# One product of 512 columns for high weights on high and low input, and one-hots made and scaled by VectorE

## The chip, the core and the metric

One of the cores of a Trainium2 chip runs the whole program. The metric is the device time of one execution in microseconds; the time before is the median of three runs. TensorE multiplies, VectorE (DVE), ScalarE (ACT) and GpSimd (POOL) do the rest, and SyncE issues the transfers. Each engine works off its own queue in order, and engines wait for each other by semaphores.

## What is computed

Two transformer blocks on 256 tokens of width 1024, in float32. The change touches the MLP of the first block and the expert layer (PEER) of the second:

```python
f = jnp.square(jax.nn.relu(u @ w_mlp_in[l])) @ w_mlp_out[l]        # 1024 -> 4096 -> 1024

# peer_ffn: 8 heads, 128 x 128 product keys, 16 experts for each head and token
experts = jnp.take_along_axis(cand_idx, pos, axis=-1)
gates = jax.nn.softmax(top_score, axis=-1)
u = jnp.take(expert_down, ei, axis=0)
act = jax.nn.gelu(jnp.einsum("btd,bthkd->bthk", xi, u), approximate=False)
y = jnp.einsum("bthk,bthkd->btd", gi * act, jnp.take(expert_up, ei, axis=0))
```

## The kernel before

**Units of weights.** All weights come in 465 units of 128 x 1024 numbers. ScalarE rounds a unit to fp32r (the high part, `WH`, `split`), and VectorE, for some units with GpSimd's help, takes the difference (the low part, `WL`). The input of a product is split in the same way; high and low part of one feature group lie side by side, 256 + 256 columns of one tile (`XW` or `GW`, seen as `XH`/`XL` and `GH`/`GL`). `products` makes three products for each of 8 steps: high weights by high input, high weights by low input, low weights by high input, each 256 columns into the same 256 columns of a bank of PSUM. A unit that has gone through sets `unit`; ScalarE or VectorE takes the result from the bank (`evac`), and later work on it is `after`.

**Order.** Every engine walks the same list of units (`SLOTS`) with a clock of four ticks per unit. At the start of a unit, ScalarE and VectorE evacuate the unit before and split the weights of the unit two ahead (`due`); smaller jobs (`..._side`) come in at a fixed unit and tick. `bank_of` says which bank a unit writes: three in turn in the MLP and for expert units 4 to 47, two in turn from expert unit 48 on. TensorE waits until the unit that had the bank before is evacuated (`bank_ready`).

**First layer of the MLP.** Units 57 to 120 (`MLP` to `XA`): 32 hidden blocks ("in") and 32 output units ("out"), four and four in turn. ScalarE takes a hidden block with ReLU, VectorE squares it, ScalarE and VectorE split it into `GH` and `GL`.

**Expert layer.** All 16384 experts are computed for every token: 128 down units (`DN` = 209 on), each giving 128 experts x 256 tokens, go through Gelu (ScalarE) into `ACTS`. During the first 46 of them VectorE is also busy with the top-k of all heads (`topk_side`), which ends with expert numbers and gates; TensorE transposes these ("ids", "gate") for `ET` and `GATE`. From `BUILD` = `DN` + 54 on, in 64 groups of four tokens, one per unit: VectorE compares keys with a counter (`build_hot_side`, both one-hots of four tokens in one operation of 1024 elements, two units ahead), ScalarE scales the second one-hot by the gates (`build_scale_side`), TensorE multiplies the two (`build_side`, four products of 128 columns after the first quarter of the unit), VectorE multiplies the finished experts by the result (`build_fold_side`, 4 x n numbers, n growing from 54 to 117), ScalarE copies it for the experts to come (`build_fill_side`), and GpSimd multiplies the newly evacuated expert unit by what has been filled (`evac`, m = 4 to 256 numbers). Then 128 up units follow with products of 512 columns.

## Time and profile before

| | |
|---|---|
| median of 3 runs | 1549.84 us (1549.16 to 1550.37) |
| the profiled execution | 1550.6 us, span 1548.8 us |
| mean granted TensorE clock | 0.992 of full speed |
| TensorE busy | 1509.2 us, 97% of the span |
| VectorE, ScalarE, GpSimd busy | 1036.5, 841.2, 366.3 us |
| first layer's MLP | about 215 to 403 us |
| expert down units with one-hots being built | about 925 to 1165 us |

The numbers of a row are the start and length of an instruction (or of a merged run of them, "x3"), its engine, the line of the kernel, the operation, what it writes and reads, and in brackets how long its engine had been idle and what ended that. A length includes a tail that overlaps the next instruction: what an instruction costs its engine is the distance to the next start. Line 1700 is VectorE's helper for operations of two tensors, 1266 ScalarE's, 684 TensorE's, 2421 GpSimd's.

### The profile page before, as it was taken

The numbers are of one execution on the slowest core, as the hardware profiler recorded it, in microseconds if no ns is written. First come the engines' busy times: TensorE is split into PE (matmuls) and PEld (weight loads), VectorE is DVE, ScalarE is ACT, GpSimd is POOL, SyncE is SP. The second block draws the span as 40 slices with busy tenths as digits, with TensorE's granted clock in tenths as the row PEclk, the third lists the DMA queues.
The fourth block names the chain that finished last, engine by engine and source line by source line (L and its number), as shares of the span: only waits on it lengthen the run. The fifth ranks groups of instructions, "written<-read, shape, count | busy, mean of one in ns | idle before, by whom it ended". The sixth has DMA issues, their size and how long they took to land.

```text
span 1548.8 us, 29248 instructions
## 1 busy us (share of the span) xinstructions
PE 1509.2 (97%) x11442; PEld 1427.7 (92%) x11442; DVE 1036.5 (67%) x1814; ACT 841.2 (54%) x1647; POOL 366.3 (24%) x397
## 2 busy tenths in 40 slices
PE   7999999999879999999999999999999999999998
PEld 7888999999879999999999999999999888888887
DVE  5666666555578764677999956777774555555554
ACT  4576465444446543554444457777774455445544
POOL 1542420000338653403555520011112000000000
PEclk9999999999999999999999999999999999999999
DMA  8652555655325632355455554444445666666664
GB/s 239 209 168 83 175 171 180 185 182 187 121 88 169 187 112 83 128 185 172 146 178 177 178 180 143 141 137 142 145 137 175 193 192 193 196 193 192 193 196 141
DMA packets 76805, 255.15 MB, mean 165 GB/s; under 512 B 9359, under 2 KB 15325, under 8 KB 76541
## 3 DMA queue, kind: packets, MB, share of 16 engines
q1 hardware_dynamic: 76429, 252.63, 52.1%
q8 instruction: 92, 1.51, 0.4%
q0 software_dynamic: 240, 0.66, 0.2%
q14 instruction: 44, 0.36, 0.1%
HBM read 250.23 MB, written 2.75 MB: 163 GB/s over the span
## 4 chain that ended last, share of the span: by engine, by line
PE 86%; DVE 10%; ACT 1%; issue 1%; POOL 1%; DMA 0%; SPq 0%; POOLq 0%; ACTq 0%; DVEq 0%
PE bank L684 85%; DVE wl L1700 3%; DVE big L1700 2%; ACT wh L1266 1%; DVE big L2266 1%; DVE big L1703 1%; DVE big L2277 1%; DVE big L2273 1%; DVE big L2262 1%; DVE big L2283 1%; DVE big L2270 1%; PE bank L1015 0%; ACT big L1266 0%; POOL wl L2421 0%; DMA big<-in_xT 0%
## 5 line engine op out<-in xcount | busy, mean ns | idle before, releaser
L1700 DVE TENSOR_TENSOR wl<-raw,wh 128x1024 fp32r<-128x1024 f32 (+4 forms) x467 | 540.1, 1158 | 379.4 <-ACT wh L1266 378.2
L1266 ACT ACTIVATE wh<-raw 128x1024 fp32r<-128x1024 f32 (+1 forms) x467 | 489.8, 1052 | 320.3 <-PE bank L684 319.2
L684 PE MATMUL bank<-gw,wh 128*128 128x256 f32 x3504 | 647.2, 286 | 0.0
L684 PEld LDWEIGHTS bank<-gw,wh 128*128 128x128 f32 x3504 | 544.7, 192 | 0.2
L684 PE MATMUL bank<-gw,wl 128*128 128x256 f32 x1752 | 495.9, 283 | 6.0 <-POOL wl L2421 5.9
L684 PEld LDWEIGHTS bank<-gw,wl 128*128 128x128 f32 x1752 | 335.2, 191 | 7.4 <-issue 6.2
L684 PE MATMUL bank<-xw,wh 128*128 128x256 f32 x1696 | 326.2, 293 | 12.2 <-ACT wh L1266 8.3
L684 PE MATMUL bank<-wh,xw 128*128 128x512 f32 x1056 | 325.3, 389 | 0.0
L684 PEld LDWEIGHTS bank<-xw,wh 128*128 128x128 f32 x1696 | 271.5, 197 | 18.9 <-ACT wh L1266 8.6
L2421 POOL TENSOR_TENSOR wl<-raw,wh 128x384 fp32r<-128x384 f32 (+4 forms) x139 | 193.7, 1401 | 303.6 <-ACT wh L1266 303.5
L1266 ACT ACTIVATE big<-bank 128x256 f32<-128x256 f32 (+22 forms) x326 | 118.0, 372 | 252.8 <-PE bank L684 213.8
L684 PE MATMUL bank<-xw,wl 128*128 128x256 f32 x848 | 244.4, 288 | 0.0
L684 PEld LDWEIGHTS bank<-wh,xw 128*128 128x128 f32 x1056 | 198.2, 188 | 41.2
L684 PE MATMUL bank<-wl,xw 128*128 128x512 f32 x528 | 205.4, 389 | 0.0
L684 PEld LDWEIGHTS bank<-xw,wl 128*128 128x128 f32 x848 | 166.8, 197 | 0.9 <-DVE wl L1700 0.9
L2421 POOL TENSOR_TENSOR big<-big 128x256 f32<-128x256 f32 (+14 forms) x116 | 106.6, 930 | 213.1 <-ACT big L1266 187.5
L684 PEld LDWEIGHTS bank<-wl,xw 128*128 128x128 f32 x528 | 99.1, 188 | 20.5
L684 PE MATMUL bank<-big 128*128 128x128 f32 (+8 forms) x952 | 98.6, 270 | 4.7 <-DVE big L1994 2.5
L2421 POOL TENSOR_TENSOR big<-big,misc 128x256 f32<-128x256 f32 (+32 forms) x74 | 37.0, 500 | 251.1 <-ACT misc L1266 251.1
L2421 POOL TENSOR_TENSOR big<-big,cols 128x8 f32<-128x8 f32 (+1 forms) x8 | 11.0, 1374 | 358.2 <-DVE big L2409 347.4
L684 PEld LDWEIGHTS bank<-big 128*128 128x128 f32 (+4 forms) x952 | 84.1, 173 | 10.8 <-issue 3.3
L1266 ACT ACTIVATE big<-big 128x256 f32<-128x256 f32 (+2 forms) x183 | 70.7, 405 | 30.3 <-DVE big L1703 15.4
(142 smaller groups left out, 1117.2 us busy)
## 6 DMA issues: line engine op xcount, KB each, us to landing
raw<-in_wst SPq DMA_DIRECT2D x455, 512.0 KB, 3.8
big<-toeplitz SPq DMA_DIRECT2D x16, 128.0 KB, 4.9
raw<-in_w1k SPq DMA_DIRECT2D x4, 512.0 KB, 4.9
raw<-in_w1v SPq DMA_DIRECT2D x4, 512.0 KB, 4.2
big<-in_xT SPq DMA_DIRECT2D x4, 256.0 KB, 5.9
raw<-in_wst SPq DMA_DIRECT2D x4, 256.0 KB, 5.1
diag_in<-big SPq DMA_DIRECT2D x2, 512.0 KB, 3.3
big<-in_keys SPq DMA_DIRECT2D x1, 1024.0 KB, 5.5
```

What stands on the lines that cost most here:

```text
L684: return e.matmul(o, a, b, start=first, stop=last, skip_group_check=True)
L1266: return e.activation(o, x, f, **kw)
L1700: return e.tensor_tensor(o, a, b, f)
L1703: return e.scalar_tensor_tensor(o, a, s, b, f, g)
L2262: e.max(v[:, 0:8], s).then_inc(*tkD.sent((h, tile, names[0][k])))
L2266: e.match_replace(x, v[:, 0:8], s, -3.0e38).then_inc(*tkD.sent((h, tile, names[1][k])))
L2270: e.max(v[:, 8:16], x).then_inc(*tkD.sent((h, tile, names[2][k])))
L2273: e.max_index(i[:, 0:8], v[:, 0:8], s).then_inc(*tkD.sent((h, tile, names[3][k])))
L2277: e.max_index(i[:, 8:16], v[:, 8:16], x).then_inc(*tkD.sent((h, tile, names[4][k])))
L2283: e.tensor_reduce(p[:, :, h, :], flat(room).rearrange("p (t k i) -> p t k i", t=2, i=16), AX, ALU.add).then_inc(*tkD.sent((h, "red", n)))
L2421: return e.tensor_tensor(o, a, b, f)
```

## The change

`WIDE` names 30 hidden blocks of the MLP (all but the first two) and the last 89 down units. For them `wide_products` makes two products per step: high weights by 512 columns (high and low input at once, into both halves of the bank), and low weights by the 256 high columns into the first half. The halves are then added: in the MLP ScalarE copies the second half, VectorE adds the first and does ReLU and square in one operation; in the expert layer ScalarE copies the second half to `LOWS` (`low_half`), splits the next weights, VectorE adds the copy into the bank, and then ScalarE's Gelu follows. `build_scale_side` is gone: VectorE makes each one-hot of 128 by itself, the second one scaled by the gate in the same operation, one unit ahead. The fold comes after the new one-hots in the order, and now waits for the fill.

```diff
+
+
+
+WIDE = [u for u in HID.values() if u >= MLP + 2] + [u for u in range(DN + 39, UP)]
...
-        HOT = [flat(XW[:, 2 * r:2 * r + 2, :]).rearrange("p (t n i) -> p t n i", n=2, i=128) for r in range(4)]
+        HOT = [XW[:, r, :].rearrange("p (t i) -> p t i", i=128) for r in range(4)]
...
+            if u in WIDE and u < XA:
+                return joined.at(u)
             return evD.at(u) if u in evD.value else evA.at(u)
...
+                def wide_products(u, x):
+
+
+                    wh, wl = WH[:, u % RW, :], WL[:, u % RW, :]
+                    o = banks[bank_of(u)]
+                    bank_ready(u)
+                    e.wait_ge(*hi.at(u))
+                    for k in range(8):
+                        c = half(k)
+                        mm(o[:, :], wh[:, c], x[:, k, :], k == 0, k == 7)
+                        if k == 0:
+                            lo_ready(u)
+                        z = mm(o[:, 0:T], wl[:, c], x[:, k, 0:T], False, k == 7)
+                        if k == 7:
+                            z.then_inc(*unit.sent(u))
+                        if k % 2:
+                            yield
+
...
+                    if u in WIDE:
+                        return wide_products(u, XW if u < XA else GW)
...
-                            e.wait_ge(*fiA.at(g - 2))
+                            e.wait_ge(*foD.at(g - 2))
                         for j in range(4):
-                            e.wait_ge(*vgA.at((g, j)))
-                            mm(b[:, half(j)], HOT[g % 4][:, j, 0, :].bitcast(F32), VG[j]).then_inc(*buP.sent((g, j)))
+                            e.wait_ge(*hotD.at((g, j, 1)))
+                            mm(b[:, half(j)], HOT[g % 4][:, j, :].bitcast(F32), VG[j]).then_inc(*buP.sent((g, j)))
...
-                        act(HT[n % 3], ps, AF.Relu).then_inc(*evA.sent(u))
+                        if u in WIDE:
+                            act(HT[n % 3], b[:, T:2 * T], AF.Copy).then_inc(*evA.sent(u))
+                        else:
+                            act(HT[n % 3], ps, AF.Relu).then_inc(*evA.sent(u))
...
-                        e.wait_ge(*unit.at(u))
+                        if u in WIDE:
+                            e.wait_ge(*joined.at(u))
+                        else:
+                            e.wait_ge(*unit.at(u))
...
+                def low_half(u):
+                    if u - 1 in lowA.value:
+                        e.wait_ge(*joined.at(u - 1))
+                    if u > BUILD:
+                        e.wait_ge(*dnG.at(u - 1 - DN))
+                    e.wait_ge(*unit.at(u))
+                    act(LOWS, banks[bank_of(u)][:, T:2 * T], AF.Copy).then_inc(*lowA.sent(u))
...
-                def build_scale_side():
-                    for g in range(NB):
-                        yield from clock.until(BUILD - 1 + g, 1)
-                        e.wait_ge(*hotD.at(g))
-                        if g == 0:
-                            e.wait_ge(*tkA.at("gate"))
-                        for j in range(4):
-                            if g:
-                                e.wait_ge(*buP.at((g - 1, j)))
-                            act(VG[j], HOT[g % 4][:, j, 1, :].bitcast(F32), AF.Copy,
-                                scale=GATE[:, 4 * g + j:4 * g + j + 1]).then_inc(*vgA.sent((g, j)))
...
-                        e.wait_ge(*foD.at(g))
+                        e.wait_ge(*buP.at((g, 3)))
...
+                    if u - 1 in lowA.value:
+                        low_half(u - 1)
+                        split(due(u))
...
+                    elif u in WIDE and u < XA:
+                        n = MLP_UNITS[u - MLP][1]
+                        x = HT[n % 3]
+                        e.wait_ge(*evA.at(u))
+                        tt(x, ps, x, ALU.add).then_inc(*joined.sent(u))
+                        e.wait_ge(*joined.at(u))
+                        stt(x, x, 0.0, x, ALU.max, ALU.mult).then_inc(*rqD.sent(n))
+                    elif u in WIDE:
+                        e.wait_ge(*lowA.at(u))
+                        tt(ps, ps, LOWS, ALU.add).then_inc(*joined.sent(u))
...
-                        e.wait_ge(*buP.at((g, 3)))
+                        e.wait_ge(*fiA.at(g))
...
                 def build_hot_side():
                     for g in range(NB):
-                        yield from clock.until(BUILD - 2 + g, 1)
+                        yield from clock.until(BUILD - 1 + g, 1)
                         if g == 0:
                             e.wait_ge(*tkA.at("ids"))
+                            e.wait_ge(*tkA.at("gate"))
                             e.wait_ge(*unit.at(DN - 1))
                         if g >= 4:
                             e.wait_ge(*buP.at((g - 4, 3)))
-                        tt(HOT[g % 4], IOTA[:, None, None, :].broadcast_to([128, 4, 2, 128]),
-                           ET[:, :, 4 * g:4 * g + 4].rearrange("p n t -> p t n")[:, :, :, None].broadcast_to([128, 4, 2, 128]),
-                           ALU.is_equal).then_inc(*hotD.sent(g))
+                        for j in range(4):
+                            t = 4 * g + j
+                            e.tensor_scalar(HOT[g % 4][:, j, :], IOTA, ET[:, 0, t:t + 1], None,
+                                            ALU.is_equal).then_inc(*hotD.sent((g, j, 0)))
+                            if g:
+                                e.wait_ge(*buP.at((g - 1, j)))
+                            e.tensor_scalar(VG[j], IOTA, ET[:, 1, t:t + 1], GATE[:, t:t + 1],
+                                            ALU.is_equal, ALU.mult).then_inc(*hotD.sent((g, j, 1)))
```

VectorE while the one-hots are being built, one unit and the start of the next, before (`big<-big,bank` is a fold, `xw<-misc` a comparison, `wl<-raw,wh` a split):

```order
1020 L1700 TENSOR_TENSOR big<-big,bank 128x59x4 [waits down_pool,ev_act,build_pe]
1021 L1700 TENSOR_TENSOR xw<-misc 128x1024 [waits build_pe]
1022 L1700 TENSOR_TENSOR wl<-raw,wh 128x1024 [waits hi]
1023 L1700 TENSOR_TENSOR big<-big,bank 128x60x4 [waits down_pool,ev_act,build_pe]
1024 L1700 TENSOR_TENSOR xw<-misc 128x1024 [waits build_pe]
```

The same place now (`bank<-bank,misc` is the addition of the halves):

```order
1127 L1733 TENSOR_TENSOR big<-big,bank 128x59x4 [waits down_pool,ev_act,fill]
1128 L1733 TENSOR_TENSOR bank<-bank,misc 128x256 [waits low_copied]
1129 L1733 TENSOR_TENSOR wl<-raw,wh 128x1024 [waits hi]
1130 L2400 TENSOR_SCALAR xw<-misc 128x128 [waits build_pe]
1131 L2404 TENSOR_SCALAR misc<-misc 128x128 [waits build_pe]
1132 L2400 TENSOR_SCALAR xw<-misc 128x128
1133 L2404 TENSOR_SCALAR misc<-misc 128x128 [waits build_pe]
1134 L2400 TENSOR_SCALAR xw<-misc 128x128
1135 L2404 TENSOR_SCALAR ones<-misc 128x128 [waits build_pe]
1136 L2400 TENSOR_SCALAR xw<-misc 128x128
1137 L2404 TENSOR_SCALAR ident<-misc 128x128 [waits build_pe]
1138 L1733 TENSOR_TENSOR big<-big,bank 128x60x4 [waits down_pool,ev_act,fill]
```

One comparison has become eight, an addition has come in, and the comparisons stand between split and fold.

ScalarE in the same stage, before (`wh<-raw` rounds weights, `xw,misc` is the scaling, `big<-bank` with three sizes the fill, the rows after it Gelu in two parts):

```order
742 L1266 ACTIVATE wh<-raw 128x1024 [waits unit,load0]
743 L1266 ACTIVATE misc<-xw,misc 128x128 [waits build_pe,hot]
744 L1266 ACTIVATE misc<-xw,misc 128x128 [waits build_pe]
745 L1266 ACTIVATE ones<-xw,misc 128x128 [waits build_pe]
746 L1266 ACTIVATE ident<-xw,misc 128x128 [waits build_pe]
747 L1266 ACTIVATE big<-bank 128x71x4 [waits fold]
748 L1266 ACTIVATE big<-bank 128x240 [waits unit]
749 L1266 ACTIVATE misc<-bank 128x16 [waits down_pool]
```

and now:

```order
781 L1294 ACTIVATE misc<-bank 128x256 [waits unit,down_pool,halves_joined]
782 L1294 ACTIVATE wh<-raw 128x1024 [waits unit,load0]
783 L1294 ACTIVATE big<-bank 128x212 [waits halves_joined]
784 L1294 ACTIVATE misc<-bank 128x44 [waits down_pool]
785 L1294 ACTIVATE big<-bank 128x63x4 [waits build_pe]
```

The four scalings are gone, a copy has come in, and Gelu moved behind the rounding of weights, where it waits for VectorE's addition.

VectorE at the end of top-k (the COPY and the `128x256` operation behind it are the maximum and the subtraction ahead of the exponential; L2283 sums expert numbers), before:

```order
990 L1700 TENSOR_TENSOR big<-big 128x512 [waits topk_pool] x2
991 L1700 TENSOR_TENSOR wl<-raw,wh 128x640 [waits hi]
992 L2321 COPY big<-big 128x16
993 L1700 TENSOR_TENSOR big<-big 128x256 [waits topk]
994 L1700 TENSOR_TENSOR wl<-raw,wh 128x640 [waits hi] x3
995 L2283 TENSOR_REDUCE big<-big 128x2x16 [waits topk_pool] x2
```

and now:

```order
1021 L1733 TENSOR_TENSOR big<-big 128x512 [waits topk_pool] x2
1022 L1733 TENSOR_TENSOR bank<-bank,misc 128x256 [waits low_copied]
1023 L1733 TENSOR_TENSOR wl<-raw,wh 128x640 [waits hi]
1024 L2364 COPY big<-big 128x16
1025 L1733 TENSOR_TENSOR big<-big 128x256 [waits topk]
1026 L1733 TENSOR_TENSOR bank<-bank,misc 128x256 [waits low_copied]
1027 L1733 TENSOR_TENSOR wl<-raw,wh 128x640 [waits hi]
1028 L1733 TENSOR_TENSOR bank<-bank,misc 128x256 [waits low_copied]
1029 L1733 TENSOR_TENSOR wl<-raw,wh 128x640 [waits hi]
1030 L1733 TENSOR_TENSOR bank<-bank,misc 128x256 [waits low_copied]
1031 L1733 TENSOR_TENSOR wl<-raw,wh 128x640 [waits hi]
1032 L2326 TENSOR_REDUCE big<-big 128x2x16 [waits topk_pool] x2
```

An addition stands ahead of each split, and each waits for ScalarE's copy.

## Rows read from the trace of the kernel before

**Rows 1.** The page: busy times by engine; chain that ended last, by engine.

```profile
PE 1509.2 (97%) x11442; PEld 1427.7 (92%) x11442; DVE 1036.5 (67%) x1814; ACT 841.2 (54%) x1647; POOL 366.3 (24%) x397
...
PE 86%; DVE 10%; ACT 1%; issue 1%; POOL 1%; DMA 0%; SPq 0%; POOLq 0%; ACTq 0%; DVEq 0%
```

**Rows 2.** Windows: us, then busy time (instructions) by engine, clock, DMA.

```profile
215.00:403.00 188.00, 187.65 (x1559) 187.29 (x1559) 110.81 (x154) 92.36 (x150) 9.63 (x12) 0.99 0.57 178
...
925.00:1165.00 240.00, 240.00 (x2042) 240.00 (x2041) 176.06 (x190) 181.94 (x506) 28.88 (x63) 1.00 0.45 141
```

**Rows 3.** Timeline of TensorE: expert down units, then up units (512 columns).

```profile
799.99 0.40 PE L684 MATMUL bank<-gw,wh 128*128 128x256 f32 x2
...
800.35 0.40 PE L684 MATMUL bank<-gw,wh 128*128 128x256 f32 x2
...
1251.65 0.84 PE L684 MATMUL bank<-wh,xw 128*128 128x512 f32 x3
...
1253.01 0.84 PE L684 MATMUL bank<-wh,xw 128*128 128x512 f32 x3
```

**Rows 4.** Timeline of VectorE, late in the build stage: one unit.

```profile
1152.71 1.23 DVE L1700 TENSOR_TENSOR wl<-raw,wh 128x1024 fp32r<-128x1024 f32 x1 [0.87 <-ACT wh L1266]
1153.85 0.62 DVE L1700 TENSOR_TENSOR big<-big,bank 128x456 f32<-128x456 f32 x1
1154.39 1.22 DVE L1700 TENSOR_TENSOR xw<-misc 128x1024 fp32r<-128x1024 f32 x1
1156.48 1.23 DVE L1700 TENSOR_TENSOR wl<-raw,wh 128x1024 fp32r<-128x1024 f32 x1 [0.86 <-ACT wh L1266]
```

**Rows 5.** Timelines of ScalarE (scalings) and GpSimd in the same stage.

```profile
1156.92 0.40 ACT L1266 ACTIVATE ones<-xw,misc 128x128 f32<-128x128 f32 x1
1157.21 0.39 ACT L1266 ACTIVATE ident<-xw,misc 128x128 f32<-128x128 f32 x1
...
1159.34 0.71 POOL L2421 TENSOR_TENSOR big<-big,misc 128x248 f32<-128x248 f32 x1 [3.06 <-ACT misc L1266]
```

**Rows 6.** Timelines of VectorE and GpSimd where they meet.

```profile
40.40 1.11 DVE L1907 TENSOR_SCALAR big<-misc 128x2 f32<-128x2 f32 x1
...
39.77 1.72 POOL L2421 TENSOR_TENSOR wl<-raw,wh 128x448 fp32r<-128x448 f32 x1 [16.51 <-ACT wh L1266]
...
887.70 3.51 POOL L2421 TENSOR_TENSOR big<-big 128x512 f32<-128x512 f32 x2 [1.14 <-DVE big L1700]
...
888.14 1.92 DVE L1700 TENSOR_TENSOR wl<-raw,wh 128x640 fp32r<-128x640 f32 x1
889.99 1.25 DVE L2321 COPY big<-big 128x16 f32<-128x16 f32 x1
```

**Rows 7.** VectorE: operations without and with pointers (timeline; last row: groups by form).

```profile
226.59 0.42 DVE L1700 TENSOR_TENSOR big<-big 128x256 f32<-128x256 f32 x1
226.92 0.76 DVE L1700 TENSOR_TENSOR gw<-big,gw 128x256 fp32r<-128x256 f32 x2
...
430.10 0.22 DVE L2093 TENSOR_SCALAR big<-bank,misc 128x8 f32<-128x8 f32 x1
430.24 0.22 DVE L1703 SCALAR_TENSOR_TENSOR big<-bank,misc,big 128x8 f32<-128x8 f32 x1
...
430.64 0.47 DVE L1703 SCALAR_TENSOR_TENSOR big<-big,cols 128x256 f32<-128x256 f32 x1
431.03 0.17 DVE L2099 TENSOR_SCALAR big<-big 128x16 f32<-128x16 f32 x1
...
L1793 DVE TENSOR_SCALAR big<-big 128x48 f32<-128x48 f32 x1 | 0.2, 190 | 2.2 <-ACT big L1266 2.2
```

**Rows 8.** End of top-k: TensorE's two waits, and ScalarE's table load.

```profile
892.30 0.35 PE L684 MATMUL bank<-gw,wl 128*128 128x256 f32 x1 [1.32 <-POOL wl L2421]
...
899.19 0.65 PE L1220 MATMUL bank<-ident,big 128*128 128x128 f32 x4 [0.43 <-DVE big L2283]
...
892.91 1.28 ACT L1266 ACT_TABLE_LOAD   x1
```

10 lines of the change are left out of this document (6 added, 4 removed).

## The prediction, made before the changed kernel ran

> **What bounds the kernel now.** I read the page first. TensorE is busy for 97% of the span and holds 86% of the chain that ended last; VectorE holds 10% of it [rows 1]. The windows by stage come next. In the first layer's MLP (215 to 403 us) TensorE fills 187.65 of 188 us, in the expert stage in which one-hots are built (925 to 1165 us) 240.00 of 240, both at the full clock (0.99 and 1.00), while VectorE is busy 110.81 and 176.06 us [rows 2]. So time there comes from what TensorE issues, as long as the other engines keep up.
>
> The timeline of TensorE gives the price of one product. Three products of 256 columns start 0.36 us apart (799.99 to 800.35), thus 120 ns each. Six of 512 columns take 1.36 us (1251.65 to 1253.01), thus 227 ns each [rows 3]. Both are their columns at 2.4 GHz (107 and 213 ns) and 13.3 ns more: that remainder is paid per product, not per column. A unit of weights is 24 products of 256 columns, 2.88 us.
>
> In the build stage one unit takes longer: VectorE's high-low splits start 3.77 us apart (1152.71, 1156.48) [rows 4], since four small products that build the expert table are in it. VectorE works off three things per unit there: a split (1.14 us to the next start), a fold (0.54), a one-hot comparison of 1024 elements (about 1.2), and then idles 0.86 us [rows 4]. ScalarE scales four one-hots (some 0.29 us apart) and GpSimd does one multiplication of up to 0.71 us [rows 5].
>
> **Term 1, the merged products: -12.7 us.** In each of 8 steps of a wide unit, 256 + 256 columns with the same high weights become 512: 240 - 227 = 13.3 ns, 8 x 13.3 = 107 ns a unit. There are 30 such units in the MLP and 89 in the expert stage: 119 x 0.107 = 12.7 us. The Trainium skill (TensorE: Matmul & The Clock Gate, Back-to-back issue gap) gives a remainder of 2.5 ns per isolated product; by it the term would be an estimated 119 x 8 x 2.5 ns = 2.4 us. The rows show 13.3 ns at both widths, and I take the rows.
>
> **Term 2, joining in the MLP: 0.** The high-by-low half now has to be added. ScalarE copies 256 columns where it took the ReLU before (same size); VectorE gets one addition more, 0.33 us (an addition of 256 starts its follower 0.33 us later, 226.59 to 226.92 [rows 7]). 30 x 0.33 = 10 us on an engine that idles 77 of 188 us [rows 2]; a bank comes round only after three hidden units and a hidden block is used four units later at the earliest. Were that cover gone, 0.33 us a unit would show.
>
> **Term 3, the end of top-k: +3.3 us (0 to 5).** Around 890 us VectorE, not TensorE, ends last. TensorE waits 1.32 us at 892.30 for GpSimd's part of a split, and 0.43 us for a reduction before the transposes of the expert numbers (899.19) [rows 8]. The order shows what is added: an addition ahead of each split in this stretch, two of them ahead of the COPY and the subtraction. The first shifts GpSimd's multiplications, so the first wait grows by 0.33 us and also swallows the 0.43 us that four wide units have saved. Then ScalarE: its Gelu now waits for the addition, which VectorE reaches only after the subtraction. Thus the table load (1.28 us), so far loaded while ScalarE waited, comes behind it, and the following copy, split and Gelu slip. Following the queues: subtraction done at 892.7, Gelu 893.4, load 894.7, exponential 895.1, copy and split 896.4, load 897.7, Gelu 898.0, next copy and split 899.3; VectorE's split then ends at 900.5, the reductions at 901.7 instead of 899.1. TensorE does its transposes at 901.8, 2.6 us later than before, where it should be 0.7 us earlier: 3.3 us. The low end holds if ScalarE's order is kinder than I think, the high end if VectorE and GpSimd block each other once more.
>
> **Term 4, VectorE in the build stage: +13 us (0 to 33).** This decides the sign. TensorE's unit shrinks to 3.77 - 0.11 = 3.66 us. Behind each other on VectorE now stand: the addition (0.33), the split (1.14), eight comparisons of 128 elements, and the fold. The fold is 0.06 us and its elements at 0.96 per ns: 216 elements at the first group (0.28), 468 at the last (0.55); the row with 456 gives 0.54 [rows 4].
>
> No row shows such a comparison, so I bound it. An operation without a pointer costs 0.06 us plus its elements (0.33 for 256 [rows 7]); with one per-partition pointer, 0.12 plus its elements (0.39 for 256; 0.14 for 8) [rows 7]. TENSOR_SCALAR within SBUF went from 0.17 to 0.19 us between 16 and 48 elements [rows 7]: half an element's time each, so 128 elements are 0.07 us. The comparison with one pointer is then 0.19 us. The second one has two pointers (key and gate). If both are fetched at once it is 0.19 too; if each adds 0.06, it is 0.25. I take 0.25, as one pointer against none shows exactly that step. Eight: 4 x 0.19 + 4 x 0.25 = 1.76 us, with 1.52 as the low end and, with no halving, 4 x 0.26 + 4 x 0.32 = 2.3 as the high end.
>
> Then the port that VectorE and GpSimd share. At 40.40 a TENSOR_SCALAR of 2 elements took 1.11 us: it ended with GpSimd's operation of 39.77 + 1.72. At 888.14 a split took 1.92 us and at 889.99 a COPY of 16 elements 1.25 us, both behind GpSimd's multiplications [rows 6]. They alternate, the waiting one gets the port. (The Trainium skill, SBUF — State Buffer, on the shared port pair as an exclusive lock, says this; the trace agrees.) GpSimd's multiplication for the unit just evacuated comes due during the split, so it goes before the first comparison. From 888.14 to 891.21 GpSimd's two operations of 512 elements had the port but for some 0.75 us of split, 1.16 us each or 2.2 ns per element [rows 6]; less the comparison's own start, which it covers, that is about 0.0022 m - 0.08 us for m elements, 0 to 252: at the end 0.47 us. Before, it fell into time in which VectorE waited.
>
> Sum per unit, group g = 0 to 63: 0.33 + 1.14 + 1.76 + fold + port = 3.52 at the first, 4.24 at the last; it passes TensorE's 3.66 at about g = 15. The mean excess of the 48 units behind that is 0.28 us: 13.6 us. VectorE may be late by some 0.6 us before TensorE's build products wait: 13.0 us. With 1.52 it is 3.28 to 4.00, 4.2 us; with 2.3, some 33 (no port held) to 46 us. Who waits: TensorE, at the four build products in the second quarter of each unit, for the one-hots. ScalarE loses 1.2 us of scaling a unit and gets a copy of 0.3 us; it cannot bind.
>
> **Sum.** 12.7 - 3.3 - 13.0 = -3.6, so 3.6 us slower. The profiled execution took 1550.6 us (span 1548.8), 0.8 us above the median 1549.84: 1554.2 on it, 1553.4 as a median. A difference under 0.2% (3.1 us) can't be told from none here.
>
> **Rivals.**
> (a) The second pointer is free: term 4 is 4.2 us, the time 1549.8 - 12.7 + 3.3 + 4.2 = 1544.6, faster. For it: in one row the pointer's cost might be mere latency of one read. Against: none is a row with two.
> (b) Small operations cost no more than those without pointers, 0.06 + 0.07 = 0.13 us, eight 1.04 us. The unit is then 2.8 to 3.5 us, always below 3.66, term 4 is zero and the time 1540.4. The Trainium skill (VectorE: DVE Perf Modes, the TRN2 errata) has 58 + FD/2 cycles for such an operation, whatever its scalars, which is this case; the same page's advice to minimize the count of operations speaks against the change. Against: pointers cost 0.06 us in every row here.
> (c) No halving, as the output is fp32r or the comparison has no such form: 33 us or more, 1573 or above. The slope between 16 and 48 elements speaks against.
> (d) A wide product does not shed the 13.3 ns, because the weights' load behind it sets the pace: term 1 is zero, and VectorE, with 3.77 us a unit, loses some 9 us: about 1562. Against: 227 ns in a stage whose products also load new weights each time.
>
> **How the numbers follow.** Likeliest case 0.46, its own range 1549 to 1560; (a) 0.22, (b) 0.13, (c) 0.08, (d) 0.04; the rest, 0.07, is a top-k end that costs far less or more. The range 1541 to 1562 leaves out (c) and half of (b). Faster by over 0.2% (below 1546.7): most of (a) and all of (b), 0.31. Within: the rest of (a) and the lower part of the first case, 0.25. Slower: 0.44.
>
> **What would show it.** Term 1: wide products 227 ns apart and narrow ones 120, units of the MLP with an inner layer 2.77 us, that stage 3.2 us shorter with TensorE still at 187 parts of 188. Term 3: the transposes' wait some 2 us instead of 0.43. Term 4: comparisons 0.19 and 0.25 us apart, VectorE without idle time from about the fifteenth build unit, TensorE waiting in the build products, units growing from 3.66 to 4.2 us at the end, the first comparison of a unit long and ending with GpSimd's operation. I am wrong if VectorE idles between units up to the end of the build stage, or if TensorE waits for its banks rather than for one-hots.

## The result, and the profile after

| | before | after |
|---|---|---|
| median | 1549.5 us (1548.14 to 1550.37, 4 runs) | 1561.62 us (1560.91 to 1563.14, 4 runs) |
| ratio of the times | | 1.0082, 95% interval 1.0070 to 1.0094 |
| span of the profiled execution | 1548.8 us | 1559.1 us |

The change costs 12.1 us. The direction was forecast, and 1561.6 lies just inside the range, but the range was 21 us wide, and of the 10.3 us by which the spans of the two profiled executions differ the forecast had only 3.6.

The page of the changed kernel, answering to [rows 1]: busy times by engine, then the chain that ended last, by engine.

```profile
PE 1514.7 (97%) x10490; PEld 1378.9 (88%) x10490; DVE 1131.3 (73%) x2381; ACT 795.6 (51%) x1480; POOL 402.3 (26%) x397
...
PE 68%; DVE 25%; issue 3%; ACT 2%; POOL 2%; SPq 0%; DMA 0%; POOLq 0%; ACTq 0%; DVEq 0%
```

TensorE issues 952 instructions fewer and is busy 5.5 us longer: a product that waits for its input in mid-stream is counted as busy. The chain tells it better: VectorE's share went from 10% to 25%.

Where the 10.3 us of span went is read between instructions of TensorE that both kernels have: the sums with a vector of ones ahead of and behind the MLP, the transposes near 713 us, the first and last build products (the small products that multiply the one-hots), and the first product of an up unit.

| stretch | before | after | change | forecast |
|---|---|---|---|---|
| start to MLP (same code) | 209.89 | 208.20 | -1.7 | 0 |
| first layer's MLP | 193.23 | 190.57 | -2.7 | -3.2 |
| from there to the transposes near 713 us | 309.97 | 309.89 | -0.1 | 0 |
| from those to the first build products | 212.72 | 215.60 | +2.9 | +1.7 |
| first to last build products (63 units) | 237.30 | 246.41 | +9.1 | +6.3 |
| the last ten down units, behind them | 31.84 | 34.60 | +2.8 | -1.1 |
| up units | 347.96 | 347.96 | 0 | 0 |

**The build stage.** Windows of the changed kernel (columns as in [rows 2]): the first interval between build products, the next 21, the other 41, and the last ten down units.

```profile
924.26:928.61 4.35, 4.35 (x27) 3.62 (x26) 4.35 (x16) 2.02 (x5) 0.00 (x0) 1.00 0.50 165
928.61:1005.73 77.12, 77.12 (x505) 69.82 (x504) 76.83 (x229) 42.75 (x105) 16.21 (x21) 1.00 0.47 142
1005.73:1170.67 164.94, 164.94 (x987) 142.41 (x986) 164.94 (x451) 80.35 (x207) 39.87 (x41) 1.00 0.42 132
1170.67:1205.27 34.60, 33.37 (x183) 27.37 (x181) 20.76 (x30) 17.85 (x36) 14.71 (x10) 1.00 0.49 157
```

VectorE is busy for 164.94 of 164.94 us in the third window. A unit takes 3.67 us in the second (77.12 / 21) and 4.02 in the third (164.94 / 41). TensorE reads as fully busy in all three, as before, so its busy share says nothing here; the busy time of its weight loads fell to 142.41 of 164.94, and that is where its waiting shows.

One unit of VectorE late in the stage, answering to [rows 4]: L2400 is the first comparison of a pair (one pointer), L2404 the second (two pointers); then fold, addition and split. Behind it GpSimd's multiplication and TensorE's build products of the same unit.

```profile
1152.38 0.71 DVE L2400 TENSOR_SCALAR xw<-misc 128x128 fp32r<-128x128 f32 x1
1153.02 0.34 DVE L2404 TENSOR_SCALAR misc<-misc 128x128 f32<-128x128 f32 x1
1153.27 0.28 DVE L2400 TENSOR_SCALAR xw<-misc 128x128 fp32r<-128x128 f32 x1
1153.47 0.34 DVE L2404 TENSOR_SCALAR misc<-misc 128x128 f32<-128x128 f32 x1
...
1154.63 0.61 DVE L1733 TENSOR_TENSOR big<-big,bank 128x448 f32<-128x448 f32 x1
1155.16 0.42 DVE L1733 TENSOR_TENSOR bank<-bank,misc 128x256 f32<-128x256 f32 x1
1155.49 1.21 DVE L1733 TENSOR_TENSOR wl<-raw,wh 128x1024 fp32r<-128x1024 f32 x1
1156.63 0.71 DVE L2400 TENSOR_SCALAR xw<-misc 128x128 fp32r<-128x128 f32 x1
```

```profile
1151.90 1.11 POOL L2470 TENSOR_TENSOR big<-big,misc 128x232 f32<-128x232 f32 x1 [3.14 <-ACT misc L1294]
```

```profile
1157.87 0.72 PE L692 MATMUL bank<-misc,xw 128*128 128x128 f32 x4
1158.55 0.49 PE L692 MATMUL bank<-ones,xw 128*128 128x128 f32 x2
1159.00 0.49 PE L692 MATMUL bank<-ident,xw 128*128 128x128 f32 x2
```

From start to start, the comparisons take 0.20 us (1153.27 to 1153.47) and 0.25 (1153.02 to 1153.27), the fold 0.53, the addition 0.33, the split 1.14, and the first comparison 0.64: GpSimd's operation ends at 1153.01, and the next comparison starts at 1153.02. From 1152.38 to 1156.63 it is 4.25 us without a gap. TensorE's build products follow the comparisons 0.45 us apart.

**The end of top-k.** TensorE's two waits in the changed kernel, answering to [rows 8], and the products behind the second.

```profile
888.12 0.35 PE L692 MATMUL bank<-gw,wl 128*128 128x256 f32 x1 [1.84 <-POOL wl L2470]
...
896.99 0.80 PE L1248 MATMUL bank<-ident,big 128*128 128x128 f32 x4 [2.30 <-DVE big L2326]
...
899.30 0.41 PE L692 MATMUL bank<-gw,wl 128*128 128x256 f32 x1
...
899.94 0.41 PE L692 MATMUL bank<-gw,wl 128*128 128x256 f32 x1
```

A wide and a narrow product take 0.64 us here (899.30 to 899.94) instead of 0.35. The windows show why: the granted clock, 1.00 up to the end of the wait, reads 0.57 in the 4 us behind it; the slow products ran at the lower of the two levels, 1.2 GHz.

```profile
894.50:897.00 2.50, 0.20 (x3) 0.01 (x1) 2.08 (x4) 1.89 (x4) 2.03 (x2) 1.00 0.67 210
897.00:901.00 4.00, 4.00 (x15) 3.50 (x16) 2.01 (x5) 0.87 (x2) 0.56 (x1) 0.57 0.63 171
```

**The last ten down units.** ScalarE, VectorE, GpSimd and TensorE in one of them (`misc<-bank` is the copy of the second half of the bank at 1184.32, and Gelu at 1185.55).

```profile
1182.72 1.51 POOL L2470 TENSOR_TENSOR big<-big,misc 128x256 f32<-128x256 f32 x1 [1.76 <-ACT misc L1294]
1184.32 0.39 ACT L1294 ACTIVATE misc<-bank 128x256 f32<-128x256 f32 x1 [1.67 <-POOL big L2470]
1184.60 1.05 ACT L1294 ACTIVATE wh<-raw 128x1024 fp32r<-128x1024 f32 x1
1184.73 0.43 DVE L1733 TENSOR_TENSOR bank<-bank,misc 128x256 f32<-128x256 f32 x1 [1.10 <-ACT misc L1294]
1185.55 0.37 ACT L1294 ACTIVATE misc<-bank 128x256 f32<-128x256 f32 x1
1185.97 0.50 PE L692 MATMUL bank<-gw,wh 128*128 128x512 f32 x1 [0.20 <-ACT misc L1294]
1186.00 1.51 POOL L2470 TENSOR_TENSOR big<-big,misc 128x256 f32<-128x256 f32 x1 [1.77 <-ACT misc L1294]
1187.59 0.39 ACT L1294 ACTIVATE misc<-bank 128x256 f32<-128x256 f32 x1 [1.67 <-POOL big L2470]
```

It is a ring of 3.27 us (1184.32 to 1187.59): copy, split, Gelu, GpSimd's multiplication, next copy. The copy waits for GpSimd, because `LOWS` is the same place as `TG`, which Gelu writes and GpSimd reads. TensorE has 2.77 us of work in that time and waits for its bank.

### The profile page after: what moved, and what is told of

Read it like the earlier page. It is cut to its first block, busy times and chain, and to the rows that moved or that the text cites. A ratio compares the mean times of both kernels' runs of the same rounds, so it can differ in the third digit from the quotient of the medians.

```text
span 1559.1 us, 27768 instructions
## 1 busy us (share of the span) xinstructions
PE 1514.7 (97%) x10490; PEld 1378.9 (88%) x10490; DVE 1131.3 (73%) x2381; ACT 795.6 (51%) x1480; POOL 402.3 (26%) x397
## 3 DMA queue, kind: packets, MB, share of 16 engines
HBM read 250.23 MB, written 2.75 MB: 162 GB/s over the span
## 4 chain that ended last, share of the span: by engine, by line
PE 68%; DVE 25%; issue 3%; ACT 2%; POOL 2%; SPq 0%; DMA 0%; POOLq 0%; ACTq 0%; DVEq 0%
PE bank L692 67%; DVE wl L1733 7%; DVE xw L2400 4%; DVE big L1733 3%; DVE bank L1733 1%; POOL big L2470 1%; ACT wh L1294 1%; DVE misc L2404 1%; DVE ones L2404 1%; DVE ident L2404 1%; DVE big L1736 1%; DVE big L2309 1%; DVE big L2320 1%; DVE big L2316 1%; ACT big L1294 1%
## 5 line engine op out<-in xcount | busy, mean ns | idle before, releaser
L692 PE MATMUL bank<-gw,wh 128*128 128x256 f32 (+1 forms) x2792 | 642.8, 316 | 1.3 <-ACT misc L1294 1.2
L692 PEld LDWEIGHTS bank<-gw,wh 128*128 128x128 f32 x2792 | 458.2, 191 | 32.7 <-ACT misc L1294 3.5
L692 PE MATMUL bank<-xw,wh 128*128 128x256 f32 (+1 forms) x1456 | 322.0, 311 | 12.8 <-ACT wh L1294 8.1
L692 PEld LDWEIGHTS bank<-xw,wh 128*128 128x128 f32 x1456 | 239.3, 195 | 30.8 <-ACT wh L1294 8.4
L2470 POOL TENSOR_TENSOR big<-big,misc 128x256 f32<-128x256 f32 (+32 forms) x74 | 73.8, 997 | 229.1 <-ACT misc L1294 229.1
L1294 ACT ACTIVATE misc<-bank 128x256 f32<-128x256 f32 (+22 forms) x165 | 56.7, 344 | 116.9 <-PE bank L692 101.2
L1733 DVE TENSOR_TENSOR big<-bank,big 128x256 f32<-128x256 f32 (+4 forms) x125 | 60.9, 495 | 47.1 <-PE bank L692 24.4
```

Of the source, the lines that this page charges most:

```text
L692: return e.matmul(o, a, b, start=first, stop=last, skip_group_check=True)
L1294: return e.activation(o, x, f, **kw)
L1733: return e.tensor_tensor(o, a, b, f)
L2470: return e.tensor_tensor(o, a, b, f)
```

## Experiments

The stretches named in what follows are those of the table. Their lengths in each kernel were read from its TensorE timeline, in one profiled execution. The times are medians.

**One-hots by ScalarE again, all products merged.** The edit takes the new one-hots out and puts the old ones back:

```diff
-                        for j in range(4):
-                            t = 4 * g + j
-                            e.tensor_scalar(HOT[g % 4][:, j, :], IOTA, ET[:, 0, t:t + 1], None,
-                                            ALU.is_equal).then_inc(*hotD.sent((g, j, 0)))
...
+                        tt(HOT[g % 4], IOTA[:, None, None, :].broadcast_to([128, 4, 2, 128]),
...
+                            act(VG[j], HOT[g % 4][:, j, 1, :].bitcast(F32), AF.Copy,
+                                scale=GATE[:, 4 * g + j:4 * g + j + 1]).then_inc(*vgA.sent((g, j)))
```

> The changed kernel with the one-hots made as before (VectorE compares 1024 elements in one operation two units ahead, ScalarE scales the second ones by the gates); all 119 merged units stay. Theory (VectorE's eight comparisons bind the build stage): VectorE's work per unit is then an addition 0.33, a split 1.14, a fold 0.28 to 0.55 and a comparison 1.2 us, 2.95 to 3.2 us, below TensorE's 3.66 us, so the 63 intervals between build products fall from 246.4 to 63 x 3.66 = 230.6 us, and no one-hot is waited for. The end of top-k and the last ten down units stay as in the changed kernel. Time: 1561.6 - 15.8 = 1545.8 us, 1544 to 1548. Rival (the chain copy, addition, Gelu and GpSimd's multiplication, or ScalarE with four scalings of 0.29 and a copy of 0.3 us more than before, sets the pace of the build stage): intervals stay above 3.9 us late in the stage and the time at 1553 us or above.

Measured: 1548.25 us, ratio 0.999 (0.9981 to 0.9999). The build stage takes 232.12 us (windows of build stage and last ten units):

```profile
927.38:1159.50 232.12, 232.12 (x1515) 210.12 (x1514) 212.63 (x252) 193.06 (x567) 69.26 (x62) 1.00 0.48 144
1159.50:1193.52 34.02, 32.65 (x183) 27.07 (x181) 19.42 (x24) 17.68 (x36) 15.01 (x10) 1.00 0.53 158
```

That is 14.3 us under the changed kernel and 5.2 under the one before: beside the merged products the eight comparisons cost 14.3 us, and the rival falls. The other two stretches kept their losses (215.63 and 34.02 us against 215.60 and 34.60), so but for 0.6 us these have nothing to do with the one-hots. A unit is 3.684 us here rather than 3.66, which is 1.5 us over 63 units, and the time is 2.4 us above what was expected. VectorE is only just covered, though. Late in the stage its comparison, with GpSimd's multiplication in its way, takes 1.65 us to the next start. With the fold (0.54), the addition (0.33) and a split of 1.14 that is 3.66 us of TensorE's 3.68:

```profile
1150.54 1.73 DVE L1746 TENSOR_TENSOR xw<-misc 128x1024 fp32r<-128x1024 f32 x1
1152.19 0.62 DVE L1746 TENSOR_TENSOR big<-big,bank 128x456 f32<-128x456 f32 x1
1152.73 0.42 DVE L1746 TENSOR_TENSOR bank<-bank,misc 128x256 f32<-128x256 f32 x1
```

**VectorE's one-hots, but no down unit merged.**

```diff
-WIDE = [u for u in HID.values() if u >= MLP + 2] + [u for u in range(DN + 39, UP)]
+WIDE = [u for u in HID.values() if u >= MLP + 2]
```

> The changed kernel with merged products in the MLP only: VectorE makes and scales the one-hots, but no expert down unit is merged, so the additions are gone. Theory (VectorE's sum of 0.33 + 1.14 + 1.76 + fold + port decides, and without the addition it is 3.93 us at the last group against TensorE's 3.77): VectorE falls behind only for the last ten or eleven units, by 0.16 us at most, under 1 us in all; the stage takes 238.2 us instead of 237.3 before and 246.4 with both parts. The time is 1548.0 (merged products in the MLP alone) + 0.9 = 1548.9 us. Rival (the comparisons bind alone, by their order or their waits for build products and fill): stage above 242 us and time above 1553 us.

Measured: 1549.74 us, ratio 1.0001 (0.9992 to 1.001). Build stage and last ten units:

```profile
920.68:1159.79 239.11, 239.11 (x2019) 238.32 (x2018) 227.56 (x632) 107.33 (x253) 59.58 (x62) 1.00 0.45 140
1159.79:1191.82 32.03, 32.03 (x268) 31.91 (x267) 16.03 (x19) 15.37 (x25) 9.00 (x11) 1.00 0.59 178
```

239.11 us against 237.30 before: 0.5 us of the difference stand in the first interval (4.25 us) and 1.3 in the last fourteen, which grow from 3.78 to 3.95. The comparisons alone cost 1.8 us in this stage, the merged units alone save 5.2, and both together cost 9.1. The two parts are not additive, since each takes from VectorE's idle 0.86 us a unit [rows 4]: the addition 0.33, the comparisons 0.56 and what they wait for GpSimd.

**The gate left out of the second comparison.**

```diff
-                            e.tensor_scalar(VG[j], IOTA, ET[:, 1, t:t + 1], GATE[:, t:t + 1],
-                                            ALU.is_equal, ALU.mult).then_inc(*hotD.sent((g, j, 1)))
+                            e.tensor_scalar(VG[j], IOTA, ET[:, 1, t:t + 1], None,
+                                            ALU.is_equal).then_inc(*hotD.sent((g, j, 1)))
```

> The changed kernel whose second comparisons have one pointer instead of two; the scaling of experts by the gates is left out, so the time is that of a kernel without it. Theory (VectorE's issue time binds from about the 22nd build unit on, and the second pointer costs 0.06 us): a unit late in the stage takes 4.26 - 4 x 0.06 = 4.02 us, VectorE falls behind at about the 38th, and the 63 intervals take about 246.4 - 9 = 237.5 us; the time is 1552.6 us. Rival (the second pointer's 0.06 us is latency of one operation that the next hides): comparisons still start 0.25 us apart and the time stays at 1561 us.

Measured: 1553.76 us, ratio 1.0029 (1.002 to 1.0038); the build stage 237.24 us. VectorE's second comparison is now followed after 0.19 to 0.20 us:

```profile
1152.41 0.28 DVE L2404 TENSOR_SCALAR misc<-misc 128x128 f32<-128x128 f32 x1
1152.61 0.27 DVE L2400 TENSOR_SCALAR xw<-misc 128x128 fp32r<-128x128 f32 x1
```

The last units take 4.02 and 4.03 us, and VectorE falls behind at about the 43rd (38th expected). So 0.06 us, four times in each of 63 intervals, are worth 9.2 us of the stage: they lie on the path and are not hidden by the next operation.

**GpSimd's multiplication cut to 4 elements.**

```diff
-                            tt(x, x, TG[:, 0:m], ALU.mult).then_inc(*dnG.sent(n))
+                            tt(x[:, 0:4], x[:, 0:4], TG[:, 0:4], ALU.mult).then_inc(*dnG.sent(n))
```

> The changed kernel with GpSimd's multiplication of the evacuated expert unit cut to 4 of its m elements (4 to 256); the products of the other elements with their factors are left out. Theory (VectorE's first comparison waits for the port that GpSimd holds, 0.0022 m - 0.08 us a unit, and the last ten units wait for GpSimd through the shared place of the low copy): the first comparison behind a split costs 0.2 instead of 0.64 us, the last build units take 3.8 instead of 4.26 us, the stage 235 us instead of 246.4; the last stretch falls from 34.6 to 31 us. Time 1561.6 - 11.3 - 3.7 = 1546.6 us, 1545 to 1550. Rival for the build stage (the 0.64 us are something else, such as the wait for the build product or a slow first access, and the growth of a unit from 3.7 to 4.3 us is the fold's alone): late units stay above 4.15 us and the time above 1555 us.

Measured: 1548.41 us, ratio 0.9991 (0.9982 to 1.0001). Build stage and last ten units, and VectorE behind a split:

```profile
926.41:1162.02 235.61, 235.59 (x1515) 211.99 (x1514) 234.75 (x696) 124.66 (x315) 44.56 (x62) 1.00 0.47 142
1162.02:1192.82 30.80, 30.80 (x182) 27.03 (x181) 20.42 (x29) 18.41 (x37) 10.13 (x11) 1.00 0.59 185
```

```profile
1153.10 0.28 DVE L2400 TENSOR_SCALAR xw<-misc 128x128 fp32r<-128x128 f32 x1
1153.29 0.34 DVE L2404 TENSOR_SCALAR misc<-misc 128x128 f32<-128x128 f32 x1
```

The first comparison takes 0.19 us instead of 0.64, the stage 10.8 us less, the last stretch 3.8 us less. Both theories about GpSimd hold, the one on the build stage and the one on the last ten units. (One of the short multiplications, at 1110.12, lasted 2.44 us for no reason that the trace shows; the two intervals next to it took 3.94 and 4.42 us, some 0.8 us of the stage.)

**The last ten down units not merged.**

```diff
-WIDE = [u for u in HID.values() if u >= MLP + 2] + [u for u in range(DN + 39, UP)]
+WIDE = [u for u in HID.values() if u >= MLP + 2] + [u for u in range(DN + 39, DN + 118)]
```

> The changed kernel with the last ten down units (those behind the last build products) not merged. Theory (a loop of ScalarE's copy, its split, Gelu and GpSimd's multiplication of 1.50 us sets 3.27 us a unit there, because the copy of the next low half waits for the multiplication): units take 2.88 us again, the stretch from the last build products to the up units falls from 34.6 to about 31.8 us, the time to 1558.8 us, give or take 0.7. Rival (the stretch is long because VectorE comes into it late from the build stage): it stays at 34 us or more and the time at 1561.6 us or 1.1 us above, since ten units lose 0.107 us each.

Measured: 1560.09 us, ratio 1.0067 (1.0051 to 1.0082). The last stretch takes 32.42 us; it was 34.60, and 31.84 before. The rival, by which it would have stayed at 34 us, falls as the main cause; the 0.6 us that are left above 31.84 can be VectorE's lateness. The time was expected at 1558.8 us, give or take 0.7, and is 0.6 us above that.

**The low half in a place of its own.**

```diff
-        LOWS = TG
+        LOWS = XW[:, 7, T:2 * T]
...
-                    if u > BUILD:
-                        e.wait_ge(*dnG.at(u - 1 - DN))
                     e.wait_ge(*unit.at(u))
...
```

> The changed kernel with the copy of the low half in a place of its own instead of the place that Gelu writes and GpSimd reads, so that the copy no longer waits for GpSimd's multiplication. Theory (this shared place closes the loop that sets 3.27 us a unit behind the last build products): the ten units there take 2.77 us, the stretch to the up units falls from 34.6 to 30.8 us, the time to 1561.6 - 3.8 = 1557.8 us; the build stage keeps its 246 us, since VectorE binds it. Rival (GpSimd's multiplication of 1.50 us with Gelu ahead of it, or VectorE's addition and split, set the pace by themselves): the stretch stays at 34 us and the time at 1561 us or more.

Measured: 1559.18 us, ratio 1.0066 (1.0051 to 1.0081). The last stretch takes 31.85 us, 2.75 less; the build stage stays at 246.55. The copy no longer waits for GpSimd, only for TensorE:

```profile
1186.55 0.39 ACT L1294 ACTIVATE xw<-bank 128x256 fp32r<-128x256 f32 x1 [1.21 <-PE bank L692]
```

The shared place closed the ring. The 1.1 us that are missing to the 30.8 expected are no wait of this kind: pairs of products start 353 ns apart in this stretch rather than 347 (0.5 us), and the unit with the last build products takes 4.29 us rather than 3.67, since VectorE comes late out of the build stage (0.6 us).

**Merged down units from the 48th on.**

```diff
-WIDE = [u for u in HID.values() if u >= MLP + 2] + [u for u in range(DN + 39, UP)]
+WIDE = [u for u in HID.values() if u >= MLP + 2] + [u for u in range(DN + 47, UP)]
```

> The changed kernel with merged down units from the 48th on rather than from the 40th, so that none meets the end of top-k. Theory (the additions ahead of the splits and Gelu behind them delay the end of top-k): the stretch from the 40th down unit to the 48th, which grew from 188.7 to 192.5 us, goes back to 188.7 us; the time is 1561.6 - 3.8 = 1557.8 us, and TensorE waits at the transposes of the expert numbers 0.4 us rather than 2.3. Rival (it is VectorE's place in the order of the one-hots, which the stretch ends with, and not the additions): the stretch stays above 191 us and the time at 1560.5 us or above.

Measured: 1559.74 us, ratio 1.0068 (1.0053 to 1.0083). The stretch to the first build products takes 212.32 us, 3.3 less than in the changed kernel. The wait at the transposes is 0.43 us, as before the change. Counted with the 0.86 us that eight merged units should save (8 x 0.107), their merging costs 4.1 us at the end of top-k. The median fell by 1.9 us only, not by the 3.8 expected. In this kernel and the two before it the medians fell by 1.9, 1.5 and 2.4 us, where the stretches of one execution each give 3.3, 2.2 and 3.8; the intervals of the ratios are 2.3 us wide to either side, so times and stretches can't be told apart here, and the argument rests on the traces.

The kernel with the low half in its own place, in this stretch the same as the changed one but for that place, shows how the sum is made up. Its stretch took 214.54 us, the changed kernel's 215.60. Its windows: up to the end of TensorE's first wait, from there to the transposes, and behind them.

```profile
884.00:889.80 5.80, 3.98 (x23) 3.19 (x22) 5.76 (x7) 1.61 (x3) 4.66 (x5) 1.00 0.31 92
889.80:898.60 8.80, 7.88 (x35) 6.58 (x35) 5.38 (x10) 7.80 (x12) 4.42 (x4) 0.81 0.61 179
898.60:903.00 4.40, 4.31 (x27) 3.85 (x28) 2.69 (x8) 2.31 (x5) 0.93 (x2) 1.00 0.61 175
```

```profile
898.69 0.66 PE L1248 MATMUL bank<-ident,big 128*128 128x128 f32 x4 [0.99 <-DVE big L2324]
```

The transposes come 8.87 us after the end of the first wait in both. Here the clock fell behind the first wait, and the slow products only filled time in which TensorE would have waited for VectorE (0.99 us left of 2.30). In the changed kernel it fell behind the second, where nothing waits any more. Why it fell behind the one wait or the other is open; in the kernel before, behind waits of 1.32 and 0.43 us, it stayed at 1.00.

**Merged products in the MLP only**, with the one-hots as before.

> The kernel before with merged products in 30 hidden blocks of the MLP and nothing else. Theory (each merged unit saves 8 x 13.3 ns = 0.107 us): 30 x 0.107 = 3.2 us, 1546.3 us. Rival (in the MLP of the changed kernel's trace a wide and a narrow product take 353 ns together from 250 us on, where 347 was expected and 360 is the price of three narrow ones): 24 units at 8 x 7 ns and 6 at 107 ns, 2.0 us, 1547.5 us. If the joining of halves costs TensorE anything there: 1549.5 us or more, with waits at the banks of the MLP.

Measured: 1547.96 us, ratio 0.9992 (0.9983 to 1.0001). The time can't tell the two apart. The trace can: from the transposes near 247 us to the sums behind the MLP it is 155.33 us before, and 154.04 or 154.05 us in this and every other kernel whose MLP units take wide and narrow products in turn, 24 merged units in this stretch. That is 0.054 us a unit, half of the 0.107 forecast. No wait is to be seen, the clock is 1.00, and narrow products keep their 0.36 us for three.

**The parts that paid, and two variants.** The first kernel takes the old one-hots and `WIDE` for the MLP and the down units 47 to 117. The second merges the last ten too, with `LOWS` in its own place. The third is the first with the products of a merged unit in another order, cut here to its main lines:

```diff
-                        mm(o[:, :], wh[:, c], x[:, k, :], k == 0, k == 7)
...
+                    for i in range(16):
+                        k = i % 8
...
+                        if i < 8:
+                            mm(o[:, :], wh[:, c], x[:, k, :], k == 0, k == 7)
```

> Only the parts of the change that paid: merged products in the MLP and in the down units from the 48th to the last with build products; one-hots compared by VectorE in one operation and scaled by ScalarE as before; the last ten down units as before. Theory (the stretches add up, since each is bound by its own engine): build stage 232.1 us against 237.3 before, the stretch ahead of it 212.3 against 212.7, the MLP 1 to 2 us shorter, the last stretch 32 us as before; 1549.3 - 5.2 - 0.4 - 1.5 = 1542.2 us, 1541 to 1543.5. Rival (the stretches do not add up, because a gain in one is given back as a wait in the next, for instance for weights): 1546 us or more, with TensorE waiting for transfers or for VectorE's low parts in the build stage.

Measured: 1542.6 us, ratio 0.9953 (0.9941 to 0.9966). Stretches: 212.29, 232.12 and 31.76 us. They add up as expected.

> As the kernel with the paying parts, but the last ten down units are merged too, with the copy of the low half in a place of its own (for which the ring of one-hots shrinks from four to three). Theory: without VectorE's eight comparisons it does not come late into the last stretch, so ten units of 2.77 us take 30.8 us instead of 31.9, and the time is 1.1 us under that of the kernel with the paying parts, 1541.1 us. Rival (with its own place the last stretch measured 31.85 us in the changed kernel, not 30.8, because GpSimd's multiplication of 1.50 us and VectorE's work take the shared port in turn): 31.9 us, no gain, 1542.2 us.

Measured: 1541.08 us, ratio 0.9948 (0.9936 to 0.996), the fastest of all. Build stage and last ten units:

```profile
921.12:1153.24 232.12, 232.12 (x1514) 210.12 (x1513) 212.58 (x253) 192.52 (x567) 69.38 (x62) 1.00 0.47 144
1153.24:1183.95 30.71, 30.71 (x182) 26.98 (x181) 20.36 (x26) 18.30 (x37) 15.81 (x11) 1.00 0.60 183
```

The last stretch is 1.05 us shorter, as the theory has it, and its pairs of products are 347 ns apart. The times of the two kernels can't be told apart, as their intervals overlap.

> As the kernel with the paying parts, but a merged unit makes its eight products of 512 columns first and its eight of 256 columns behind them, instead of one of each in turn. It asks why a pair takes 353 ns in the MLP and 347 in the expert stage. Theory (the longer pace comes from the alternation of wide and narrow products): wide products start 227 ns apart and narrow ones 120 ns apart, eight pairs take 2.77 us in the MLP too, where they take 2.83 now, and 24 to 30 units save 0.05 us each, 1.3 to 1.6 us in all: 1540.8 us. Rival (the longer pace has another cause, such as the input's place in memory): still 2.82 to 2.83 us a unit in the MLP, and the time is that of the kernel with the paying parts, 1542.2 us.

Measured: 1542.21 us, ratio 0.995 (0.9937 to 0.9963). The time can't be told from the first kernel's. In the trace a merged unit of the MLP takes 2.80 us (252.52 to 255.32), between the 2.77 forecast and the 2.83 of alternating products, and the stretch of 24 units 153.24 us instead of 154.04.

```profile
252.52 2.00 PE L693 MATMUL bank<-xw,wh 128*128 128x512 f32 x8
254.36 1.12 PE L693 MATMUL bank<-xw,wl 128*128 128x256 f32 x8
255.32 2.00 PE L693 MATMUL bank<-xw,wh 128*128 128x512 f32 x8
```

Wide products are 230 ns apart and narrow ones 120. Of the 1.3 us that were missing in this stretch the grouped order gives back 0.8. In the build stage it costs 0.56 us (232.68 against 232.12). No run here tells why.

## Why the prediction was right or wrong

The mechanism that decided the sign, term 4, held. Two steps of the prediction failed. The first is the path behind the last build products: the prediction let ScalarE go with "it cannot bind", and there a ring through ScalarE and GpSimd held TensorE to 3.27 us a unit (3.3 us, and 3.9 with VectorE's lateness). The second is the size of term 1: a merged unit saved 0.054 us in the MLP and 0.083 in the build stage instead of 0.107 (2.8 us). Term 3 lacked what the lower clock costs behind the wait (1.5 us).

**Term 1, merged products (-12.7): about 2.8 us short.** Between the transposes of the gates and the first build products the changed kernel's profiled execution gave what was forecast: 23.98 to 23.11 us over some eight units, 0.109 each. The kernels with the low half in its own place and with merging from the 48th unit on took 23.54 and 23.57 us there, half of that gain. In the MLP 24 of 30 units gave 0.054. (That stretch of the table misses only 0.5 us, since in the profiled execution of before TensorE's clock was 0.69 from 209 to 220 us and after 1.00, outside those 24 units.) In the build stage a unit went from 3.767 to 3.684 us (the kernel with ScalarE's scaling), 0.083, which is 1.5 us less than forecast over 63 units. The step that failed was to take the 227 ns between products that are all wide [rows 3] for products that alternate with narrow ones. Rival (d), by which nothing is saved, had a part of it. Why the pace differs stays open: grouping the products gave back only 0.8 of 1.3 us in the MLP.

**Term 2, joining in the MLP (0): right.** No bank was waited for.

**Term 3, the end of top-k (+3.3): 4.1, counted as above.** The queues followed came out well. Counted from the marker at 713.09 us (708.66 after), the transposes were forecast at 188.7 us and came at 188.3, 2.2 us later than before the change; the forecast said 2.6. The wait was forecast as some 2 us and was 2.30. What the sum left out is what a wait of that length does behind itself: the granted clock fell, and the 2.64 us of products between the transposes of expert numbers and of gates took 4.16 (896.99 to 901.15), 1.5 us more. The merged units in that stretch gave back 0.9. 2.2 + 1.5 - 0.9 is the 2.9 us of the table. The runs in which the clock fell earlier, in time that was waited anyway, lost 1.1 to 1.6 us less. (The Trainium skill, TensorE: Matmul & The Clock Gate, Part 1: The HAM clock gate, says that TensorE's clock falls when it idles and comes back only with work. The trace agrees in that: the clock reads 1.00 up to the end of the wait, 0.57 from 897 to 901 us and, with TensorE at work, 1.00 from 901 to 905.)

**Term 4, VectorE in the build stage (+13.0): 14.3.** Mechanism, place and prices were right. Forecast against measured: comparisons 0.19 and 0.25 us against 0.20 and 0.25, addition 0.33 against 0.33, fold 0.55 against 0.55 at the end, port 0.47 against 0.45, period at the end 4.24 against 4.25 to 4.30. VectorE ran out of idle time where the forecast had it, at about the 15th unit: the split at 959.05 still comes 0.40 us after its addition, which takes 0.33, but from 977.48 to 981.17 its work fills 3.69 us without a gap. TensorE's intervals grow only from the 23rd (3.76 us), since VectorE's unit grows slowly (3.75 us at 1003.48) and it had some lead: from the 15th to the 22nd unit it loses 0.3 us in all against TensorE's 3.68. Of the 14.3 us 0.7 stand in the first interval (4.35 us). There VectorE has eight comparisons for the first group and eight for the second within one unit, with no lead; the sum had given VectorE a slack of 0.6 us instead. Rival (a) fell with the 0.25 us in the trace and the kernel without the gate, (b) and (c) with the 0.20 us of a comparison with one pointer, where they had 0.13 and 0.26.

**What the sum did not contain: +3.9 us in the last ten down units.** The forecast was -1.1, the measured change +2.8. The prediction said of ScalarE that it "cannot bind", from its busy time, and never followed the ring through the wait of `low_half` for GpSimd's multiplication, though the wait stands in the diff. Behind the last build products a unit of TensorE is only 2.77 us, shorter than the ring's 3.27, which is made up of copy 0.28, split 0.95, Gelu to GpSimd's start 0.45, multiplication 1.51, and the step to the next copy 0.08. The multiplication takes 1.51 us; one of 248 elements took 0.71 before the change [rows 5]. It starts 0.32 us into VectorE's split (at 1185.68, a split being worth 1.14 us) and ends 0.69 us after it, so it seems to get the port only then; with 4 elements it still lasts 0.96 us. Of the 3.9 us the ring has 3.3: the stretch takes 34.02 us with it and 30.71 without, where VectorE was not late (one-hots by ScalarE, with the shared place and with a place of its own). The other 0.6 (34.60 against 34.02 us) go with VectorE's comparisons, which leave it late. This is the largest single miss.

**What cancels.** 1.7 us of the profiled execution's span were gained ahead of the MLP, where nothing was changed. This is luck of one execution: the same stretch took 208.0 to 211.0 us in the experiments. It is about the 1.8 us by which the difference of the medians (12.1) exceeds that of the spans (10.3).

Misses in the spans, measured less forecast: MLP +0.5, top-k +1.2, build +2.8, last stretch +3.9, start -1.7, together +6.7, from the forecast 3.6 to the measured 10.3.

## What to carry to other kernels

When a change adds work to an engine with idle time, write the sum of its queue per unit, add every part of the change to it together, and look for the unit where it crosses the pace of the bottleneck: here the comparisons alone cost 1.8 us, the merged products alone gave 5.2, and both together cost 9.1. Follow each new wait around until it comes back to its own engine, with the pace of every stage that it runs through; a shared scratch buffer that is harmless at 3.7 us a unit was the bound at 2.8. And where TensorE comes to wait some 2 us, look at the granted clock behind the wait: here it cost another 1.5 us, unless a later wait took that up.

## What the hardware showed that I had not expected

A wide and a narrow product in turn have two paces, at the same full clock and with no idle time: 347 ns, the sum of 227 and 120, and 353 ns. In the changed kernel the merged units of the MLP from 249 us on run at 353. The down units before TensorE's wait at 888 us run at 353 too, and those behind it at 347. Wide products two pairs apart, first near 300 us, then near 910 us (the rows round to 0.01 us; over seven pairs it is 2.47 to 2.48 and 2.42 to 2.44 us):

```profile
299.91 0.40 PE L692 MATMUL bank<-xw,wh 128*128 128x512 f32 x1
...
300.62 0.40 PE L692 MATMUL bank<-xw,wh 128*128 128x512 f32 x1
```

```profile
910.04 0.40 PE L692 MATMUL bank<-gw,wh 128*128 128x512 f32 x1
...
910.73 0.40 PE L692 MATMUL bank<-gw,wh 128*128 128x512 f32 x1
```

A pace lasts for many units and is not tied to the input's buffer: in the kernel with the fastest time the down units ahead of the build stage run at 353 and the last ten at 347, and the kernel with the low half in its own place has 353 in the last ten. It mostly changes where a wait or other products come in between, but not only there: in the kernel with merged products in the MLP alone the first merged unit (222.44 us) runs at 347 and the one right behind it at 353. Three narrow products kept 360 ns throughout. What sets the pace stays open.

The second surprise is GpSimd's multiplication of 4 elements, which takes 0.96 us in the last ten units, where it starts 0.31 us into VectorE's split, and from 0.62 us up in the build stage. By its length it waits for the port there, which no run here tests by itself.
